# Two softmax attentions of a two-block network: add and maximum in one VectorE operation, the sink as a 257th score, value blocks on GpSimd

## The reference

```python
# neighbourhood attention: 16 queries of a column block see 256 keys
s = einsum(q, k) * dh ** -0.5
s = where(mask, s + bias, -1e30)
o = einsum(softmax(s), v)

# sliding window: 128 queries of a block see its own and the previous 128 keys
s = where(valid, einsum(q, k) * 64 ** -0.5, -1e30)
p = softmax(concatenate([s, sink], -1), -1)[..., :-1]
o = einsum(p, v)
```

## Time and profile before

| | |
|---|---|
| median of 3 runs | 3208.03 us (3198.69 to 3209.45) |
| the profiled execution | 3214.49 us |
| its span, first to last instruction | 3212.7 us |
| mean granted TensorE clock | 0.972 of full speed |
| busy share: PE, DVE, ACT, POOL | 95%, 33%, 30%, 36% |
| first attention, first to last add | 176.9 to 225.6 us |
| second attention, first to last add | 2664.3 to 2752.2 us |

### The profile page before, as it was taken

One profiled execution on the slowest core, in us unless ns is written; L12 is line 12 of the kernel. 1 busy time (PEld: TensorE's weight loads), 2 busy tenths in 40 slices (PEclk: granted clock), 3 DMA queues, 4 the chain that ended last, 5 costly groups with the idle time before them and its releaser, 6 DMA issues.

```text
span 3212.7 us, 49162 instructions
## 1 busy us (share of the span) xinstructions
PE 3037.9 (95%) x20804; PEld 2432.7 (76%) x20804; DVE 1074.9 (33%) x1482; ACT 966.5 (30%) x1206; POOL 1170.3 (36%) x331
## 2 busy tenths in 40 slices
PE   7979999999999967899999999999999997899998
PEld 6748778887888855769998788886888865678886
DVE  4450342223211147224453411116211247441213
ACT  3243232222222227432332322224222236532222
POOL 4304444443444441332331344443444440234444
PEclk9979999999999978999999999999999999999999
DMA  4202222222222222241111222222222220112222
GB/s 178 87 13 92 92 80 101 95 92 92 89 94 92 92 79 99 111 149 33 43 47 35 79 92 91 104 92 79 92 92 93 101 83 15 53 67 104 91 92 79
DMA packets 42571, 271.82 MB, mean 85 GB/s; under 512 B 4736, under 2 KB 4864, under 8 KB 12704
## 3 DMA queue, kind: packets, MB, share of 16 engines
q1 hardware_dynamic: 39312, 252.64, 22.3%
q10 hardware_dynamic: 3088, 16.65, 1.3%
HBM read 254.58 MB, written 14.68 MB: 84 GB/s over the span
## 4 chain that ended last, share of the span: by engine, by line
issue 60%; PE 18%; POOL 16%; DVE 4%; DVEq 1%; POOLq 0%; ACT 0%; ACTq 0%
POOL w_lo L478 15%; PE ps L759 8%; PE ps L587 3%; PE ps L588 2%; PE ps L589 2%; PE ps L674 1%; DVE small L1563 1%; POOL x_res L555 1%; DVEq L1562 1%; DVE work L1422 0%; PE ps L681 0%; DVE work L1505 0%; PE ps L651 0%; DVE ybuf L1578 0%; DVEq L1502 0%
## 5 line engine op out<-in xcount | busy, mean ns | idle before, releaser
L478 POOL TENSOR_TENSOR w_lo<-w_raw,w_hi 128x2048 fp32r<-128x2048 f32 x220 | 1024.1, 4655 | 1730.5 <-ACT w_hi L1000 1721.0
L587 PE MATMUL ps<-act_hi,w_hi 128*128 128x512 f32 x2240 | 895.0, 400 | 42.2 <-DVE act_lo L1450 23.2
L588 PE MATMUL ps<-act_lo,w_hi 128*128 128x512 f32 x2240 | 888.7, 397 | 0.0
L589 PE MATMUL ps<-act_hi,w_lo 128*128 128x512 f32 x2240 | 888.4, 397 | 0.0
L1000 ACT CAST w_hi<-w_raw 128x2048 fp32r<-128x2048 f32 x219 | 417.3, 1906 | 1038.9 <-PE ps L589 1014.8
L587 PEld LDWEIGHTS ps<-act_hi,w_hi 128*128 128x128 f32 x2240 | 424.9, 190 | 156.0 <-POOL w_lo L478 26.7
L589 PEld LDWEIGHTS ps<-act_hi,w_lo 128*128 128x128 f32 x2240 | 424.7, 190 | 100.5
L588 PEld LDWEIGHTS ps<-act_lo,w_hi 128*128 128x128 f32 x2240 | 424.9, 190 | 100.1 <-issue 1.7
L587 PE MATMUL ps<-hid_hi,w_hi 128*128 128x512 f32 x1184 | 470.4, 397 | 10.3 <-POOL w_lo L478 8.3
L589 PE MATMUL ps<-hid_hi,w_lo 128*128 128x512 f32 x1184 | 467.8, 395 | 0.0
L588 PE MATMUL ps<-hid_lo,w_hi 128*128 128x512 f32 x1120 | 442.6, 395 | 0.0
(11 more groups left out here) (255 smaller groups left out, 2447.7 us busy)
## 6 DMA issues: line engine op xcount, KB each, us to landing
w_raw<-stream SPq DMA_DIRECT2D x224, 1024.0 KB, 4.8
spill<-work ACTq DMA_DIRECT2D x5, 2048.0 KB, 6.3
scratch<-spill SPq DMA_DIRECT2D x24, 256.0 KB, 4.3
work<-bias_in SPq DMA_DIRECT2D x1, 3072.0 KB, 19.2
work<-spill SPq DMA_DIRECT2D x12, 256.0 KB, 3.2
x_res<-x_in SPq DMA_DIRECT2D x2, 1024.0 KB, 8.4
spill<-area ACTq DMA_DIRECT2D x4, 512.0 KB, 4.8
area<-spill SPq DMA_DIRECT2D x7, 256.0 KB, 3.0
```

Of the source, the lines that this page charges most:

```text
L478: tt(w_lo[:, s, :], w_raw[:, s, :], w_hi[:, s, :].bitcast(F32), ALU.subtract).then_inc(S["lo_made"], 1)
L587: mm(out, wh, hi[:, k, :], start=(k == 0) if begin is None else begin, stop=False)
L588: mm(out, wh, lo[:, k, :], start=False, stop=False)
L589: return mm(out, wl, hi[:, k, :], start=False, stop=end)
```

## The change

- VectorE's add and maximum become one operation per head (`tensor_tensor_reduce`): it writes the sum of scores and mask and puts the maximum of the row beside it. The second attention's rows have 257 columns: the 257th score is the sink, which TensorE writes into column 256 of the score bank with a product of the identity, in steps 0 and 1 of each four (each bank keeps it for the step two later); the mask has a 257th column of zero. The sink's own maximum, exponentials and sum are gone.
- A new semaphore, `at_added`, frees the score banks right after the reduction. The negation moves behind a wait for the exponentials of two steps before.
- ScalarE no longer copies the value blocks; GpSimd does, in a loop of its own before it goes on with the slabs, two buffers.
- The rows have four buffers, the reciprocals four. The value transposes and the row transposes come in turn `t` for step `t - 3`, the output products for step `t - 4`, so each attention has one turn more.
- A warming product stands behind the scores of steps 0 to 3 in both attentions.
- ScalarE loads the exponential's table ahead of both attentions.
- The scaling of the rows stays with VectorE and the copy of the outputs with ScalarE.

The diff, cut to its core:

```diff
@@ swa_masks
+    table = np.zeros((P, 2, 257), np.float32)
+    table[:, :, 0:256] = np.stack([np.where(ok & (s >= 128), 0, MASKED), np.where(ok, 0, MASKED)], 1)
@@ buffers
-        p_buf = yflat[:, 1536:3072].rearrange("p (b h k) -> p b h k", b=3, h=2)
+        p_buf = yflat[:, 0:2056].rearrange("p (b h k) -> p b h k", b=4, h=2)
+        NEG_MAX, SUM, MAX, RECIP = 12, 16, 20, 24
+        KEYS = (256, 257)
@@ gpsimd
+            def value_blocks():
+
+                for t in range(STEPS[0]):
+                    tile, j = divmod(t, 4)
+                    if t >= 2:
+                        pool.wait_ge(S["at_vt"], t - 1)
+                    v = work[:, 8 + tile, :].rearrange("p (r c) -> p r c", c=64)[:, :, NA_KEY0[j]:NA_KEY0[j] + 32]
+                    nc.gpsimd.tensor_copy(vb_buf[:, t % 2, :].rearrange("p (r c) -> p r c", c=32), v).then_inc(S["at_vblk"], 1)
...
             lo(0, 0)
-            done = 1
+            split(1, FIRST["conv_branch"] + 1)
+            pool.wait_ge(banks_free[1], 6)
+            value_blocks()
+            done = FIRST["conv_branch"] + 1
@@ tensor, attention
-                            pe.wait_ge(S["at_max"], g0 + t - 1)
+                            pe.wait_ge(S["at_added"], g0 + t - 1)
                         for h in range(2):
+                            out = ps[:, SCORE_BANKS[t % 2] + h, :]
+                            if a == 1 and t % 4 < 2:
+                                mm(out[:, 256:257], c("ident"), sinks[:, 2 * (t // 4) + h:2 * (t // 4) + h + 1], start=True, stop=True)
...
-                        if a == 1 and t < 3:
-                            stay_warm(1, bank=5)
...
+                        if t < 4:
+                            stay_warm(1, bank=5 if a else 4)
+                    if 3 <= t <= steps + 2:
+                        u = t - 3
...
-                    if t >= 3:
-                        u = t - 3
+                    if t >= 4:
+                        u = t - 4
                         pe.wait_ge(S["at_ptsb"], g0 + u + 1)
+                        if a == 0:
+                            pe.wait_ge(S["at_vtok"], u + 1)
                         if u:
                             pe.wait_ge(S["at_osb"], g0 + u)
@@ scalar, attention
                     if t < steps:
-                        g, b, e = g0 + t, t % 3, t % 2
-                        act.wait_ge(S["at_max"], g + 1)
+                        act.wait_ge(S["at_max"], g0 + t + 1)
+                        if t >= 2:
+                            act.wait_ge(S["at_recip"], g0 + t - 1)
                         for h in range(2):
...
+                            p = p_buf[:, t % 4, h, 0:KEYS[a]]
+                            inst = af(p, p, ACT.Exp, bias=tiny(NEG_MAX, t)[:, h:h + 1], accum_out=tiny(SUM, t)[:, h:h + 1])
...
+            preload(ACT.Exp)
             evacuated(12)
             attention(0)
@@ vector, attention
-                        tt(p_buf[:, t % 3, :, :], ps[:, SCORE_BANKS[b]:SCORE_BANKS[b] + 2, 0:256], heads_bias(t), ALU.add)
+                        for h in range(2):
+                            inst = nc.vector.tensor_tensor_reduce(p_buf[:, t % 4, h, 0:KEYS[a]], ps[:, SCORE_BANKS[t % 2] + h, 0:KEYS[a]],
+                                                                  heads_bias(t)[:, h, :], 1.0, 2 * MASKED, ALU.add, ALU.max,
+                                                                  tiny(MAX, t)[:, h:h + 1])
+                        inst.then_inc(S["at_added"], 1)
                         dve.drain()
-                        nc.vector.tensor_reduce(small[:, 20 + 2 * b:22 + 2 * b], p_buf[:, t % 3, :, :], AX_X, ALU.max)
-                        dve.drain()
-                        if a == 1:
-                            tt(small[:, 20 + 2 * b:22 + 2 * b], small[:, 20 + 2 * b:22 + 2 * b], sinks[:, 2 * (t // 4):2 * (t // 4) + 2], ALU.max)
-                            dve.drain()
...
+                        if t >= 2:
+                            dve.wait_ge(S["at_exp"], g0 + t - 1)
+                        ts(tiny(NEG_MAX, t), tiny(MAX, t), -1.0, None, ALU.mult).then_inc(S["at_max"], 1)
+                    if 1 <= t <= steps:
+                        u = t - 1
+                        dve.wait_ge(S["at_exp"], g0 + u + 1)
+                        if u >= 4:
+                            dve.wait_ge(S["at_p"], g0 + u - 3)
+                        nc.vector.reciprocal(tiny(RECIP, u, 4), tiny(SUM, u)).then_inc(S["at_recip"], 1)
```

More of the change, by code:

```diff
@@ L701, in attention @@
                 g0, steps = 16 * a, STEPS[a]
-                for t in range(steps + 3):
-                    if a == 1 and t == 2:
+                for t in range(steps + 4):
+                    if a == 1 and t == 3:
                         pe.wait_ge(banks_free[1], FIRST["o2"] // 2)
@@ L1137, in attention @@
                 g0, steps = 16 * a, STEPS[a]
-                for t in range(steps + 3):
-                    if a == 0 and 1 <= t <= steps:
-                        u = t - 1
-                        tile, j = divmod(u, 4)
-                        if u >= 2:
-                            act.wait_ge(S["at_vt"], u - 1)
-                        v = work[:, 8 + tile, :].rearrange("p (r c) -> p r c", c=64)[:, :, NA_KEY0[j]:NA_KEY0[j] + 32]
-                        nc.scalar.copy(vb_buf[:, u % 2, :].rearrange("p (r c) -> p r c", c=32), v).then_inc(S["at_vblk"], 1)
+                for t in range(steps + 4):
                     if t < steps:
-                        g, b, e = g0 + t, t % 3, t % 2
-                        act.wait_ge(S["at_max"], g + 1)
+                        act.wait_ge(S["at_max"], g0 + t + 1)
+                        if t >= 2:
+                            act.wait_ge(S["at_recip"], g0 + t - 1)
                         for h in range(2):
-                            inst = af(p_buf[:, b, h, :], p_buf[:, b, h, :], ACT.Exp,
-                                      bias=small[:, 12 + 2 * e + h:13 + 2 * e + h],
-                                      accum_out=small[:, 16 + 2 * e + h:17 + 2 * e + h])
-                        if a == 1:
-                            for h in range(2):
-                                inst = af(small[:, 24 + 2 * e + h:25 + 2 * e + h],
-                                          sinks[:, 2 * (t // 4) + h:2 * (t // 4) + h + 1], ACT.Exp,
-                                          bias=small[:, 12 + 2 * e + h:13 + 2 * e + h])
+                            p = p_buf[:, t % 4, h, 0:KEYS[a]]
+                            inst = af(p, p, ACT.Exp, bias=tiny(NEG_MAX, t)[:, h:h + 1], accum_out=tiny(SUM, t)[:, h:h + 1])
                         inst.then_inc(S["at_exp"], 1)
-                    if a == 0 and 1 <= t <= steps:
-                        u = t - 1
+                    if a == 0 and 3 <= t <= steps + 2:
+                        u = t - 3
                         act.wait_ge(S["at_vt"], u + 1)
@@ L1164, in attention @@
                         nc.scalar.copy(vt_buf[:, u % 2, :, :], ps[:, 5, 0:256].rearrange("p (a k) -> p a k", a=2)).then_inc(S["at_vtok"], 1)
-                    if 2 <= t <= steps + 1:
-                        u = t - 2
+                    if 3 <= t <= steps + 2:
+                        u = t - 3
                         act.wait_ge(S["at_pt"], g0 + u + 1)
@@ L1388, in _ @@
             root("mixer1_pre")
-            act.dma_start(work[:, 18, :].rearrange("p (b k) -> p b k", b=2), swa_in).then_inc(S["swa_loaded"], 16)
+            act.dma_start(swa_mask, swa_in).then_inc(S["swa_loaded"], 16)
             for n in range(1, 4):
                 hi_next(FIRST["q2"], n // 2, n % 2)
+            preload(ACT.Exp)
             act.wait_ge(S["vtok_mm"], 1)
@@ L1564, in attention @@
-                        dve.drain()
-                        if a == 1:
-                            tt(small[:, 20 + 2 * b:22 + 2 * b], small[:, 20 + 2 * b:22 + 2 * b], sinks[:, 2 * (t // 4):2 * (t // 4) + 2], ALU.max)
-                            dve.drain()
-                        ts(small[:, 12 + 2 * b:14 + 2 * b], small[:, 20 + 2 * b:22 + 2 * b], -1.0, None, ALU.mult).then_inc(S["at_max"], 1)
-                    if t >= 1:
-                        g, b = g0 + t - 1, (t - 1) % 2
-                        dve.wait_ge(S["at_exp"], g + 1)
-                        if a == 1:
-                            tt(small[:, 16 + 2 * b:18 + 2 * b], small[:, 16 + 2 * b:18 + 2 * b], small[:, 24 + 2 * b:26 + 2 * b], ALU.add)
-                            dve.drain()
-                        nc.vector.reciprocal(small[:, 28 + 2 * b:30 + 2 * b], small[:, 16 + 2 * b:18 + 2 * b])
+                        dve.wait_ge(S["at_s"], g0 + t + 1)
```

52 lines of the change are left out of this document (24 added, 28 removed).

## The result

The changed kernel's median is 3180.5 us (6 runs, 3177.1 to 3191.5) against 3209.5 us for the kernel before (6 runs beside them, 3198.7 to 3216.2): 0.9913 of the time, 95% interval 0.9893 to 0.9933, so 22 to 34 us less. The forecast was 20.7 us less. The profiled execution took 3191.5 us with a span of 3189.7, the slowest of its six; against the profiled one of before it is 23.0 us shorter. By the medians the gain is 29.0 us, so the 20.7 are nearer to this pair of profiles than to the medians.

What follows compares the result with a forecast made beforehand. VectorE bounded the second attention, a two-step ring the first. Gains of 9.4 and 13.6 us less 1.0 and 1.3 for the ends gave 20.7 us, so the median 3208.03 us becomes 3187; range 3171 to 3201.

Steps and rivals of the forecast that it cites:

- X: VectorE's two fused add-and-maximum reductions per step, both attentions: 1.1 us in place of 1.52 from add to next small operation.
- Rival 1: Fused reduction on VectorE runs at the scan's rate, 1.6 us for two; 10.3 us gained, 3198 us; chance 0.18.
- rival 3: Fused reductions cost over 1 us each on VectorE, so the change loses; 3234 us; chance 0.07.
- The second attention's ring: Second attention, two-step loop through output products, reduction, exponentials and ScalarE's copies: 4.51 us, half 2.26 a step before sinks.
- The sink as a column: Second attention: relieves VectorE and ScalarE; adds 0.25 us on PE per sink step (range 0 to 0.5), 0.06 per period.
- extra round at the end: End of each attention: one more round after the last exponential because of the added stage, costing 1.0 us each.
- The first attention's ring: First attention, two-step loop now over the copy of the turned values: 4.91 us, half 2.46 a step.
- Rival 2: Stages overlap fully and PE's 2.05 us a step sets the pace in both attentions; 3171 us; chance 0.13.
- Its start: First attention's first four periods, with warming products partly at the lower clock: 2.8 us each, 11.2 in all.
- Rival 4: TensorE's clock stays low through more of the first attention, its 11 remaining periods 3.2 us; 3199 us; chance 0.04.
- GpSimd beside VectorE: First attention: GpSimd's value-block copies hold the shared port against VectorE; at most 9.3 us, nearly all covered, 1 us taken.
- Block term: First attention: value blocks move to GpSimd, taking ScalarE's copy off the ring; with the port cost, 9.4 us gain.

Runs made afterwards that it cites:

- the repeated run: The changed kernel profiled once more with no edit; median 3182.8 us, 0.9927 of before; attentions 43.1 and 87.7 us.

## Why the prediction was right, and where its terms were off

**The operation.** X was put at 1.1 us and measured 0.87 to 0.88, with 257 columns as with 256 (0.85 in the kernel with the operation alone). Two terms of it were too large: the second reduction starts 0.35 after the first, not 0.42 (nor the 0.5 of "What would show it"), and the accumulator's 0.08 lies beside the next one. "VectorE: DVE Perf Modes" of the Trainium skill, section "Two Vector instructions with no wait between them", has it that an accumulator write is an instruction of its own; the trace agrees on its form, a row of its own for each. The 0.24 us that the prediction lent it from the small operations was too much, and so the 1.4 for X didn't come. Rival 1 (the scan's rate, X = 1.6) and rival 3 (X from 2.05 up) are refuted by the same row.

**The second attention's ring.** Put at 2.26 without the sinks; with X at 0.87 in the same sum it is (4.51 - 0.23)/2 = 2.14. Measured without sinks: 2.16. The ring is right to 0.02 us.

**The sink as a column is the step that failed.** The prediction took "0.25" us a step with sinks out of a range from 0 to 0.5, and 0.06 of it on the period. Measured on PE it is 1.90 - 0.66 = 1.24 us a step, over twice the upper end, and 2.60 - 2.16 = 0.44 us on the period. The sum counted the product and the load that are added. What wasn't seen is what they stand between: the products of two heads, 64 rows each, run beside each other, and a product between them, of one row as of 128, ends that. The trace of before did show it, eight score products of 64 rows in about the time of four transposes of 128 rows, in the step of the earlier trace rows:

```profile
2705.88 0.72 PE L711 MATMUL ps<-work 64*128 64x128 f32 x8
2706.90 0.66 PE L731 MATMUL ps<-cst,ybuf 128*128 128x128 f32 x4 [0.29 <-DVE ybuf L1578]
```

PE then is the bound, which also is why "2.40" with its play for three close engines came out as 2.60 on average. Of the 12.3 us forecast, 4.5 arrived in the profile, 8.4 in the repeated run. The 1.0 for the extra round at the end was about right as a cost (8.7 against 7.5 us with the sinks as before), but the prediction didn't count that the last add and maximum get shorter too, and so the tail came out even, 8.1 against 8.2.

**The first attention's ring.** Put at 2.46, measured 2.36; the same sum with the measured X is 2.34. Two more terms were off and about cancel: negation to exponential takes 0.30 instead of 0.20 (199.93 - 199.63, beside GpSimd), and the copy of the turned values to the transposes 0.40 instead of 0.49 (201.33 - 200.93). The prediction read the old ring rightly as 6.30 us for two steps, but not the ring of 3.03 without VectorE close below it. There the operation alone would have stopped, and the extra stage is what undoes it. Rival 2, a pace of 2.05, is refuted in both attentions: in the first the bank and the copies hold, as the earlier trace rows said, and in the second PE's own work does.

**Its start** was put at 11.2 us and took 9.9 and 8.8; the warming products ran at the lower level only at first:

```profile
174.64 2.07 PE L672 MATMUL ps<-cst 128*128 128x512 f32 x2
...
180.47 1.12 PE L672 MATMUL ps<-cst 128*128 128x512 f32 x2
```

Two passes in 2.07 us and later in 1.12, the two levels of the earlier trace rows. Rival 4, a clock that stays low, didn't come: it was 1.00 from 184.6 on.

**Its tail** was put at 1.0 us more than before and took 2.8 us less (8.3 against 11.1). The extra round counted is there, but the stretch that it is part of ran partly at the lower level before (0.64) and doesn't now. The tail before:

```profile
225.70:236.80 11.10, 7.33 (x49) 5.18 (x49) 3.00 (x10) 5.43 (x18) 0.00 (x0) 0.64 0.01 2
```

PE had 7.3 us of work at 0.64 there and has 6.4 at 1.00 now. The prediction priced the round and took the tail's clock as given. The last add and maximum are shorter too (0.65 us). The clock of the tail was 1.00 in every run with the new staging; why it holds was not tried by itself.

**GpSimd beside VectorE** was given 1 us in the first attention and costs about 0.6 (16 periods of 0.04). What was feared is there and small: GpSimd's copy lasts 0.41 us, and the negation that starts within it ends 0.03 after it (199.90 against 199.87) and takes 0.1 more than without it. But the Block term went wrong on the other side: with the value blocks back on ScalarE, the ring is as short. There ScalarE still copies a block at the head of its turn, as before, but that of step t - 2 instead of t - 1. So it is the extra stage that took the copy off the ring (both the ring of two steps and that of 3.03), and not the other engine; a kernel that moves the copies to GpSimd without the extra stage was not tried.

**The total** was right because two misses cancel: 7.3 us too little in the first attention, 7.8 too much in the second, and some 2 us more that arise before the first reduction. It was forecast by terms that were off by nearly 8 us each, so that it came out is luck. Two executions of the changed kernel differ by 4 us in the second attention alone: by the repeated run the second attention misses by 3.9 us instead of 7.8, and by the medians the total is 29.0, 8.3 more than forecast.

**What carries the gain** depends on the attention. In the second it is the operation (13.9 us alone, 10.7 of them in the 27 steady periods). The staging adds nothing there (83.5 against 82.2 us, the sinks handled as before in both), and the sinks as written take back 4 or more. In the first it is the rest of the change, which has 11.2 us without the operation, while the operation alone has 5.4 and only 1.2 of them in the periods. Of that rest, the warming products, GpSimd's copies and the early table gain nothing by their own experiments; so the deeper staging is left (with `at_added`), which was not tried alone.

## What to carry to other kernels

Before a product is slipped into a sequence of small ones, see whether the trace shows the neighbours running beside each other (eight records in the time of four): a product between them costs the overlap, with one row as with 128 here, and moved ahead of them costs only itself. Before a shortened ring is priced, look for the next ring close below it: here 3.03 us stood under 3.15. When VectorE leaves the bound, price what was added to the next engine by its own rows, not as slack. And a total that is met proves little: the stages should be compared one by one, and more than one execution looked at, since the clock at a stage's start moved these by 4 us with no edit at all.

## What the runs showed of the hardware that was not expected

- Score products of two heads, 64 rows each, run beside each other: 8 records in 0.66 us. With a product between the heads 4 records take 0.63. A 1x1 product does it as well as one of 128 rows.
- A product of one column costs 0.31 us on PE with its load, for 128 rows as for one. A pair of 128 rows costs 0.53, a pair of one row each, in different halves of the rows, 0.31.
- The fused add and maximum of 257 columns with one source in PSUM takes 0.42 us, a second behind it starts 0.35 later, and the read of the accumulator (0.08) hides beside it.
- A copy of 128x256 on GpSimd takes 0.41 us, and a VectorE operation of 128x2 that starts within it 0.27 instead of 0.17 (in 11 of 16 steps; 0.17 in all 16 without the copies).
- The start of the second attention ran at a granted clock of 0.68 in one execution of the changed kernel and 1.00 in another, 13.3 against 9.3 us for the same 53 products.
